# 96 instead of 80 row-gathered tokens, a ring of eight, and modulation products on four column groups

## Chip, cores and metric

One core of a Trainium2 chip runs the whole program. Times are device microseconds (us) of one execution; the kernel before takes 2507.22 us, the median of three runs (2506.68 to 2508.7). Engines are named as in the profile: PE (TensorE matmul), PEld (its weight loads), DVE (VectorE), ACT (ScalarE), POOL (GpSimd), SP (SyncE, which here only issues DMAs). A matmul of f32 operands stands in the trace as two records. All data is f32.

## What is computed

A first block (batch 1, 256 tokens, width 1024, with 256 context tokens), and then two layers of a second one. Cut to what matters here:

```python
# first block
s_lat, s_ctx = silu(c), silu(c_ctx)                    # two vectors of 1024
mod  = s_lat @ w_mod + b_mod                           # 1024 x 6144: shift, scale, gate, twice
cmod = s_ctx @ w_mod + b_mod
h = rms_norm(x) * (1 + sc1) + sh1                      # then projections, attention, Hyena, MLP
...
# each layer of the second block ends in peer_ffn
q = xn @ wq                                            # 8 heads x 2 x 128
scores = q . sub_keys;  top 16 of each half, top 16 of the 256 sums -> idx, gate (t, 8, 16)
act = einsum('td,thkd->thk', x, u_tab[idx])            # u_tab, v_tab: 16384 experts x 1024
y   = einsum('thk,thkd->td', gelu(act) * gate, v_tab[idx])
```

Each token uses 128 of the 16384 experts. Nothing else in the reference is touched by the change.

## The kernel before, in words

**The expert layer.** It is computed in two ways at once. The first TD = 176 tokens go the dense way on PE: all 16384 experts are multiplied with them, first `expert_scores` (u table, 128 expert blocks of 128, taken in 64 pairs, each pair 2 x 8 products of a 128x128 weight block with 176 columns), then `expert_values` (v table, 32 weight tiles of four blocks, 32 products of 176 columns each). The weights are streamed by SP in 2 MB tiles through three slots (`stream`, issued when the tile three places back was used up). A dense gate matrix comes from one-hot products: `gate_tiles(n)` makes the gates of BATCH = 4 tokens in four 128-column products, `onehots` (DVE) and `gate_onehots` (ACT) make their operands, `gates_out` (ACT), `gate_first` and `gate_second` (DVE) apply them. These run beside the pairs from pair FIRST_GATED = 20 on. A pair's PSUM bank is one of four and is freed by `gate_second`.

The last ROW_TOKENS = 80 tokens go the sparse way. POOL gathers rows with indirect DMAs (`gathers`): one gather brings 128 rows of 4 KB (16 tokens x 8 heads, one of the 16 choices), 80 of the u table and then 80 of the v table per layer, into a ring of RING = 6 buffers; gather m waits until the row work m - 6 is done. DVE makes a dot product of each u row set (`row_dots`, line 1892) and a scaled sum of each v row set (`row_sums`, line 1941). The dots stand in DVE's program between the gate work: DOTS_BEFORE = 12 before the first `onehots`, then DOTS_NUM / 2 = 1.5 for each pair, the rest at the end. The sums come after all gate work. `row_values(g)` lets PE add the sums of 16 tokens (eight products of 16 columns) between the tiles of the v stage. POOL's program is: the row tokens out and spread, the indices through DRAM (`move(0)`), the first RING + 2 gathers, the gates through DRAM (`move(1)`, it waits for DVE's `gate_ready`), all other gathers.

**The modulation.** w_mod is streamed in twelve 2 MB tiles. `modulation_rows(t)` makes eight products (one for each 128 rows of the contraction) of the two silu vectors (2 columns of weights) with 512 columns, all into partitions 0 and 1 of one PSUM bank. ACT copies them out (`modulation_row`), and `modulation_columns(t)` turns them with four transposes (line 481), which DVE takes (`modulation`). Tiles 0 to 3 stand at the start, 4 to 6 before the attention (behind `hy5`), 7 to 11 inside the attention loop at steps 0, 3, 6, 9 and 12. The order of work on each engine is written out by hand and does not depend on times.

The lines of the ring and the row dots:

```python
if m >= RING:
    pool.wait_ge(rows_used, m - RING + 1)
...
upto = min(ROWS, DOTS_BEFORE + (m + 1 - FIRST_GATED) * DOTS_NUM // 2)
row_dots(dots, upto - dots)
```

Of the kernel before, what the change touches and what calls it, by code (L numbers as in the profile page):

```python
# [19 lines left out]
ALU = mybir.AluOpType  # L20
# [5 lines left out]
P = 128  # L26
D = 1024
# [33 lines left out]
ROW_TOKENS = 80  # L61
# [4 lines left out]
RING = 6  # L66
# [5 lines left out]
ARENA = 46272  # L72
# [3 lines left out]
DOTS_BEFORE, DOTS_NUM = 12, 3  # L76
# [76 lines left out]
def build(nc, ins, out):  # L153
    ctx = ExitStack()
    with ctx:
# [21 lines left out]
        def const(n):  # L177
            c_at[0] += n
            return KON[:, c_at[0] - n:c_at[0]]
# [6 lines left out]
        SELG = const(GTOK)  # L186
        ZT = const(T)
        rstd = sb("rstd", [P, 2, T])
        small = sb("small", [P, 256])
# [18 lines left out]
        CE = take(KC, 2)  # L208
        MOD = take(48, 2)
# [62 lines left out]
        a_at[0] = wa_at + HALF * TD  # L272
# [7 lines left out]
        BA, BB, BP, BV, BI, BJ, GATE, EIDX = (take(TB * NSEL) for _ in range(8))  # L280
        assert a_at[0] <= wa_at + XTILES * TD
# [6 lines left out]
        XNS = view(wa_at + 48 * TD, D)  # L288
# [41 lines left out]
        def mod_rows(t):  # L330

            return SQF[0:2, 3072 + (t % 2) * 512:3584 + (t % 2) * 512] if t >= MODS_BEFORE_ATTENTION else \
                view(kt_at + A_COLS, 1024)[0:2, (t % 2) * 512:(t % 2 + 1) * 512]
# [23 lines left out]
        def _(pe):  # L357
# [110 lines left out]
            def modulation_rows(t):  # L468
                tile, w = weights(ins["w_mod"][t], KC * 512)
                w = w.rearrange("p (k n) -> p k n", k=KC)  # L470
                ps = begin(f"modr{t}")
                for k in range(KC):
                    last = mm(ps[0:2, :], CE[:, k, :], w[:, k, :], k == 0, k == KC - 1)
                used_up.append(tile)
                end(last, f"modr{t}")

            def modulation_columns(t):
                jobs.wait_read(pe, f"modr{t}")
                ps = begin(f"mod{t}")
                for j in range(4):  # L480
                    last = pe.transpose(ps[:, 2 * j:2 * j + 2], mod_rows(t)[:, j * P:(j + 1) * P],
                                        IDENT[0:2, 0:2])
# [456 lines left out]
        def _(act):  # L939
# [31 lines left out]
            def modulation_row(t):  # L971
# [3 lines left out]
                act.activation(mod_rows(t), bank(f"modr{t}")[0:2, :], ACT.Copy).then_inc(free(f"modr{t}"), 1)  # L975
# [292 lines left out]
        def _(dve):  # L1268
# [34 lines left out]
            dve.tensor_tensor(CE[:, :, :], CE[:, :, :], CS[:, :, :], ALU.mult).then_inc(s("silu_c_ready"), 1)  # L1303
# [823 lines left out]
def _constants():  # L2127
# [6 lines left out]
    for h in range(MLH):  # L2134
# [5 lines left out]
    rope = [x.reshape(TB, P, 32).transpose(1, 0, 2).reshape(P, TB * 32) for x in (np.cos(ang), np.sin(ang))]  # L2140
    iota = np.broadcast_to(np.arange(P, dtype=f), (P, P))
# [8 lines left out]
                             *rope, iota, selg, zt], axis=1).astype(f)  # L2150
# [72 lines left out]
```

## Time and profile before

| | |
|---|---|
| median of three runs | 2507.22 us |
| the profiled execution, own time | 2501.63 us |
| its span (first to last instruction) | 2499.8 us |
| PE busy | 2379.0 us (95%) |
| DVE, ACT, POOL busy | 1149.7, 454.4, 359.7 us |
| granted PE clock, mean | 0.962 of full |
| moved by DMA | 581.53 MB, mean 233 GB/s |

The span has these stretches: the first block up to 608 us (its modulation tiles in the first 330), then two layers of some 940 us. In the first of them the pairs of the u stage start at 883.6 us, the first gate product stands at 986.6, the v stage runs from 1232.8 to 1546.1; the second layer repeats this 942 us later. Busy shares are means over stages with different limits, so the stages are read one by one, and for each the question is which wait ends last there.

### The profile page before, as it was taken

Reading aid. Unit: us, or ns where it says so; the run is one execution under the profiler, and the core shown is the slowest. Engines: PE = TensorE matmul, PEld = TensorE weight load, DVE = VectorE, ACT = ScalarE, POOL = GpSimd, SP = SyncE. Lnnn points to the kernel's source line nnn. Section 1 sums busy time; section 2 is a strip of 40 time slices with the busy share of each in tenths; the row PEclk is TensorE's granted clock in tenths of the full one; section 3 lists DMA queues with packets and bytes.
Section 4 is the critical chain, followed back from the end, with each engine's and each line's share of the span. In section 5 each row is a group of like instructions: output and inputs, shape, how many; then the busy total and the mean of one; then the engine's idle time right before and its main releaser. Section 6 shows DMA issues by size and latency. Waiting matters only on the chain.

```text
span 2499.8 us, 32384 instructions
## 1 busy us (share of the span) xinstructions
PE 2379.0 (95%) x13376; PEld 2088.1 (84%) x13376; DVE 1149.7 (46%) x2391; ACT 454.4 (18%) x1076; POOL 359.7 (14%) x344
## 2 busy tenths in 40 slices
PE   6999879998989999999999998989999999999998
PEld 2464468887667899999999998667899999999998
DVE  2144422112532597667644410632597667644410
ACT  1112221000232112443200000232112443200000
POOL 0000000000000012333433300000012333433300
PEclk9999999999987999999999999987999999999999
DMA  8124222443421377989999973431368989899973
GB/s 314 66 88 183 101 85 101 152 152 128 157 101 51 135 270 297 340 316 346 332 410 409 409 264 119 165 126 51 127 229 325 336 315 345 331 407 409 409 283 118
DMA packets 103983, 581.53 MB, mean 233 GB/s; under 512 B 9145, under 2 KB 9529, under 8 KB 85786
## 3 DMA queue, kind: packets, MB, share of 16 engines
q1 hardware_dynamic: 55578, 403.31, 41.5%
q0 software_dynamic: 47968, 174.02, 19.1%
q8 instruction: 108, 1.77, 0.3%
q10 hardware_dynamic: 288, 2.10, 0.2%
q14 instruction: 41, 0.34, 0.0%
HBM read 577.52 MB, written 1.87 MB: 232 GB/s over the span
## 4 chain that ended last, share of the span: by engine, by line
PE 92%; DVE 2%; ACT 2%; DMA 2%; issue 1%; POOL 0%; POOLq 0%; SPq 0%; DVEq 0%; ACTq 0%
PE psum L387 90%; PE psum L422 1%; DMA arena<-in_w_mod 1%; DMA bounce<-arena 1%; DMA arena<-in_peer_u,small 1%; ACT HT L1074 0%; DVE rstd L1621 0%; DVE arena L1474 0%; POOL arena L2036 0%; POOLq L2009 0%; DVE XT L1993 0%; SPq L2062 0%; ACT arena L1156 0%; ACT arena L1159 0%; ACT arena L1150 0%
## 5 line engine op out<-in xcount | busy, mean ns | idle before, releaser
L387 PE MATMUL psum<-arena 128*128 128x176 f32 (+6 forms) x6154 | 1053.2, 334 | 22.1 <-DVE arena L1744 9.6
L387 PE MATMUL psum<-HT,arena 128*128 128x176 f32 (+1 forms) x5984 | 1043.2, 335 | 14.8 <-DVE HT L1623 7.1
L387 PEld LDWEIGHTS psum<-HT,arena 128*128 128x128 f32 x5984 | 972.4, 191 | 66.7 <-issue 16.7
L387 PEld LDWEIGHTS psum<-arena 128*128 128x128 f32 (+1 forms) x6154 | 913.7, 192 | 132.2 <-issue 108.3
L1941 DVE SCALAR_TENSOR_TENSOR arena<-arena,small 128x1024 f32<-128x1024 f32 x150 | 192.8, 1285 | 214.2 <-DMA arena<-in_peer_v,small 214.0
L2036 POOL DMA_INDIRECT arena<-in_peer_u,small x160 | 188.1, 1175 | 407.1 <-DVE small L1892 374.7
L387 PE MATMUL psum<-arena,HT 128*128 128x384 f32 (+3 forms) x544 | 199.2, 527 | 18.1 <-ACT HT L1003 11.1
L1892 DVE CUSTOM_DVE_ANT_0 arena<-arena 128x1024 f32<-128x1024 f32 x160 | 191.0, 1220 | 18.9 <-DMA arena<-in_peer_u,small 17.3
L2036 POOL DMA_INDIRECT arena<-in_peer_v,small x160 | 158.7, 992 | 257.0 <-DVE arena L1941 230.6
L387 PEld LDWEIGHTS psum<-arena,HT 128*128 128x128 f32 x544 | 106.8, 198 | 104.1 <-issue 42.4
L951 ACT ACTIVATE arena<-psum 128x512 f32<-128x512 f32 (+6 forms) x130 | 64.9, 513 | 693.5 <-PE psum L422 355.9
L2042 POOL DMA_DIRECT2D row_tokens<-arena x2 | 1.3, 640 | 1275.6 <-ACT arena L951 1275.6
L1228 ACT ACTIVATE arena<-arena 128x128 f32<-128x128 f32 x352 | 112.3, 390 | 170.9 <-DVE arena L1901 170.9
L1901 DVE TENSOR_TENSOR arena<-arena,KON 128x1024 f32<-128x1024 f32 x88 | 107.0, 1217 | 0.0
L387 PE MATMUL psum<-arena,KON 128*128 128x256 f32 (+5 forms) x252 | 73.3, 441 | 26.9 <-ACT arena L1099 16.8
L387 PEld LDWEIGHTS psum<-arena,KON 128*128 128x128 f32 (+1 forms) x252 | 55.0, 241 | 48.1 <-ACT arena L1099 17.3
L1993 DVE TENSOR_TENSOR XT<-psum,XT 128x512 f32<-128x512 f32 x8 | 5.0, 683 | 189.4 <-PE psum L387 189.4
L1916 DVE TENSOR_TENSOR arena<-psum,arena 128x168 f32<-128x168 f32 (+21 forms) x88 | 65.4, 743 | 51.6 <-ACT arena L1235 50.7
L1575 DVE TENSOR_SCALAR arena<-psum,arena 128x256 f32<-128x256 f32 x22 | 12.0, 544 | 167.4 <-PE psum L387 167.0
L1099 ACT ACTIVATE arena<-XT 128x512 f32<-128x512 f32 x16 | 9.4, 623 | 394.7 <-POOLq L2009 340.7
L1927 DVE TENSOR_TENSOR arena<-psum,arena 128x352 f32<-128x352 f32 (+41 forms) x86 | 30.4, 354 | 106.4 <-ACT arena L1218 97.7
L1218 ACT ACTIVATE arena<-psum 128x352 f32<-128x352 f32 (+20 forms) x124 | 44.7, 361 | 164.6 <-PE psum L387 164.6
(225 smaller groups left out, 986.5 us busy)
## 6 DMA issues: line engine op xcount, KB each, us to landing
arena<-in_peer_ut SPq DMA_DIRECT2D x64, 2048.0 KB, 8.4
arena<-in_peer_v SPq DMA_DIRECT2D x64, 2048.0 KB, 16.4
arena<-in_w_mod SPq DMA_DIRECT2D x12, 2048.0 KB, 8.1
arena<-in_w_in SPq DMA_DIRECT2D x16, 1536.0 KB, 6.2
arena<-in_w_up SPq DMA_DIRECT2D x11, 2048.0 KB, 8.0
arena<-in_peer_wq SPq DMA_DIRECT2D x8, 2048.0 KB, 7.2
arena<-in_w_out SPq DMA_DIRECT2D x6, 2048.0 KB, 7.3
arena<-in_w_down SPq DMA_DIRECT2D x11, 1024.0 KB, 4.8
```

Of the source, the lines that this page charges most:

```text
L387: return pe.matmul(o, a, b, start=start, stop=stop, skip_group_check=True)
L422: last = pe.transpose(ps[0:rows, j * P:(j + 1) * P], part, IDENT)
L951: act.activation(dst, src, ACT.Copy).then_inc(psum_free[jobs.where[name][0]], 1)
L1218: last = act.activation(WA[:, 2 * m:2 * m + 2, done:TD], ps[:, :, done:TD], ACT.Gelu_apprx_tanh)
L1228: last = act.activation(rows, rows, ACT.Copy, scale=SELT[:, 2, at:at + 1])
L1575: steps(dve.tensor_scalar(a, src, col("fcw", FC + c), col("fcb", c), ALU.mult, ALU.add))
L1892: dve.tensor_tensor_reduce(out=GR[j], in0=GR[j], in1=XNG[:, g % 2, :], scale=1.0, scalar=0.0, op0=ALU.mult, op1=ALU.add, accum_out=ACTV[:, ...
L1901: dve.tensor_tensor(OH[:, 2 * (n % 2):2 * (n % 2) + 2, :, :], bc(SELT[:, 0:2, at:at + BATCH].unsqueeze(3), P, 2, BATCH, P), bc(IOTA.unsque ...
L1916: dve.tensor_tensor(w, ps[:, :].rearrange("p (x i) -> p x i", x=BATCH)[:, :, 0:2 * m], w, ALU.mult).then_inc(free(f"g{n}"), 1)
L1927: dve.tensor_tensor(w, ps[:, :, 0:done], w, ALU.mult).then_inc(free(f"u{m}"), 1)
L1941: dve.scalar_tensor_tensor(y, GR[j], w, y, ALU.mult, ALU.add).then_inc(rows_used, 1)
L2036: pool.indirect_dma_start(out=GR[j], out_offset=None, in_=rows, in_offset=bass.IndirectOffsetOnAxis(ap=EG[:, n:n + 1].bitcast(U32), axis=0 ...
```

## The change

Three constants of the row work move: ROW_TOKENS 80 to 96 (so TD 176 to 160, six row groups instead of five, 96 gathers of each table and layer, and 40 gate groups instead of 44), RING 6 to 8, DOTS_NUM 3 to 4 (two dots a pair). Buffers move to make room. The modulation products use four column groups of PE: the silu vectors are padded to 32 columns (`CE4`), product k goes to columns and PSUM partitions 32 (k mod 4) on, so that two products add up in each group, and the four partial sums are added when the rows are turned: `modulation_columns` multiplies all 128 partitions with a 0/1 matrix `PAIR` of two columns.

```diff
-ROW_TOKENS = 80
+ROW_TOKENS = 96
-RING = 6
+RING = 8
-DOTS_BEFORE, DOTS_NUM = 12, 3
+DOTS_BEFORE, DOTS_NUM = 12, 4
...
+        PAIR = const(2)
...
-        small = sb("small", [P, 256])
+        small = sb("small", [P, 3 * ROWS])
...
+        CE4 = take(KC, 32)
...
-            return SQF[0:2, 3072 + (t % 2) * 512:3584 + (t % 2) * 512] if t >= MODS_BEFORE_ATTENTION else \
-                view(kt_at + A_COLS, 1024)[0:2, (t % 2) * 512:(t % 2 + 1) * 512]
+            return SQF[:, 3072 + (t % 2) * 512:3584 + (t % 2) * 512] if t >= MODS_BEFORE_ATTENTION else \
+                view(kt_at + A_COLS, 1024)[:, (t % 2) * 512:(t % 2 + 1) * 512]
...
                 for k in range(KC):
-                    last = mm(ps[0:2, :], CE[:, k, :], w[:, k, :], k == 0, k == KC - 1)
+                    q = 32 * (k % 4)
+                    last = pe.matmul(ps[q:q + 32, :], CE4[:, k, :], w[:, k, :], start=k < 4, stop=k >= KC - 4,
+                                     tile_position=(0, q))
...
                 for j in range(4):
-                    last = pe.transpose(ps[:, 2 * j:2 * j + 2], mod_rows(t)[:, j * P:(j + 1) * P],
-                                        IDENT[0:2, 0:2])
+                    last = mm(ps[:, 2 * j:2 * j + 2], mod_rows(t)[:, j * P:(j + 1) * P], PAIR, j == 0, True)
...
-                act.activation(mod_rows(t), bank(f"modr{t}")[0:2, :], ACT.Copy).then_inc(free(f"modr{t}"), 1)
+                act.activation(mod_rows(t), bank(f"modr{t}")[:, :], ACT.Copy).then_inc(free(f"modr{t}"), 1)
...
-            dve.tensor_tensor(CE[:, :, :], CE[:, :, :], CS[:, :, :], ALU.mult).then_inc(s("silu_c_ready"), 1)
+            steps(dve.memset(CE4[:, :, :], 0.0))
+            dve.tensor_tensor(CE4[:, :, 0:2], CE[:, :, :], CS[:, :, :], ALU.mult).then_inc(s("silu_c_ready"), 1)
```

PE at the start of the program, the four modulation tiles before the attention's projections, before the change:

```order
L387 MATMUL psum<-arena 2x512 x8
L387 MATMUL psum<-KON,arena 64x256
L387 MATMUL psum<-arena 2x512 x8
L481 MATMUL psum<-KON,arena 128x2 x4
L387 MATMUL psum<-arena 2x512 x8
L481 MATMUL psum<-KON,arena 128x2 x4
L387 MATMUL psum<-arena 2x512 x8
L481 MATMUL psum<-KON,arena 128x2 x8
```

The same place after the change:

```order
L476 MATMUL psum<-arena 32x512 x8
L389 MATMUL psum<-KON,arena 64x256
L476 MATMUL psum<-arena 32x512 x8
L389 MATMUL psum<-KON,arena 128x2 x4
L476 MATMUL psum<-arena 32x512 x8
L389 MATMUL psum<-KON,arena 128x2 x4
L476 MATMUL psum<-arena 32x512 x8
L389 MATMUL psum<-KON,arena 128x2 x8
```

Nothing moved: each product of 2 rows became one of 32 rows in its own column group, and the transposes became plain products.

POOL in one layer, from the index move to the first v gathers, before (L2036 is a gather, L2014 and L2017 the two halves of a move through DRAM, L2023 the spread of a group's tokens):

```order
L2036 DMA arena<-in_peer_u,small 128x1024 x8
L2014 DMA bounce<-arena 80x128
L2017 DMA small<-bounce 128x5x16
L2036 DMA arena<-in_peer_u,small 128x1024 x13
L2023 DMA arena<-row_tokens 128x1x1024
L2036 DMA arena<-in_peer_u,small 128x1024 x16
```

After (L2040, L2018, L2021 and L2027 are the same four):

```order
L2040 DMA arena<-in_peer_u,small 128x1024 x10
L2018 DMA bounce<-arena 96x128
L2021 DMA small<-bounce 128x6x16
L2040 DMA arena<-in_peer_u,small 128x1024 x13
L2027 DMA arena<-row_tokens 128x1x1024
L2040 DMA arena<-in_peer_u,small 128x1024 x16
```

Ten gathers instead of eight now stand ahead of the gate move.

DVE at the first gate groups of a layer, before (L1892 a row dot in two instructions, L1901 `onehots`, L1916 `gate_first`, L1927 `gate_second`):

```order
L1901 TENSOR_TENSOR arena<-arena,KON 128x1024 x2
L1916 TENSOR_TENSOR arena<-psum4,arena 128x4x42
L1901 TENSOR_TENSOR arena<-arena,KON 128x1024
L1916 TENSOR_TENSOR arena<-psum5,arena 128x4x42
L1901 TENSOR_TENSOR arena<-arena,KON 128x1024
L1891 REGISTER_ALU
L1892 ISA arena,small<-arena 128x1024
L1892 ISA small 128x1
L1927 TENSOR_TENSOR arena<-psum1,arena 128x2x8
L1916 TENSOR_TENSOR arena<-psum6,arena 128x4x44
```

After (L1896, L1905, L1920 and L1931 are the same four):

```order
L1905 TENSOR_TENSOR arena<-arena,KON 128x1024 x2
L1920 TENSOR_TENSOR arena<-psum4,arena 128x4x42
L1905 TENSOR_TENSOR arena<-arena,KON 128x1024
L1896 ISA arena,small<-arena 128x1024
L1896 ISA small 128x1
L1896 ISA arena,small<-arena 128x1024
L1896 ISA small 128x1
L1931 TENSOR_TENSOR arena<-psum1,arena 128x2x4
L1920 TENSOR_TENSOR arena<-psum5,arena 128x4x44
L1905 TENSOR_TENSOR arena<-arena,KON 128x1024
```

One gate group instead of two stands behind pair 20, and every pair carries two dots where it carried one or two in turn.

## Rows read from the trace of the kernel before

**Rows 1.** The page, part 4: the chain that ended last, share of the span by engine.

```profile
PE 92%; DVE 2%; ACT 2%; DMA 2%; issue 1%; POOL 0%; POOLq 0%; SPq 0%; DVEq 0%; ACTq 0%
```

**Rows 2.** Windows: PE, PEld, DVE, ACT, POOL busy (count), PEclk, DMA share, GB/s.

```profile
221.40:329.00 107.60, 93.94 (x404) 47.76 (x404) 49.16 (x136) 29.86 (x70) 0.00 (x0) 0.97 0.26 98
986.60:1232.80 246.20, 246.19 (x1728) 246.19 (x1729) 167.81 (x256) 97.85 (x300) 78.11 (x68) 0.99 0.89 331
1232.80:1448.00 215.20, 215.20 (x1457) 215.20 (x1455) 103.81 (x93) 1.09 (x6) 77.13 (x78) 1.00 1.02 406
```

**Rows 3.** Groups by form, PE, first 620 us: records | busy us, mean ns.

```profile
L387 PE MATMUL psum<-arena 128*2 128x512 f32 x192 | 85.9, 602 | 3.7 <-DMA arena<-in_w_mod 3.7
```

**Rows 4.** Timeline of PE, start of program: start us, length, records [idle before].

```profile
23.12 8.72 PE L387 MATMUL psum<-arena 128*2 128x512 f32 x16 [3.68 <-DMA arena<-in_w_mod]
...
46.94 7.03 PE L387 MATMUL psum<-arena 128*2 128x512 f32 x16
...
66.75 13.13 PE L387 MATMUL psum<-arena,HT 128*128 128x384 f32 x32 [11.12 <-ACT HT L1003]
```

**Rows 5.** Line 2071, landing of the third w_mod tile (issued 7.2) and fourth (31.9).

```profile
DMA to landing us min/median/max: 25.6/25.6/25.6
...
DMA to landing us min/median/max: 8.1/8.1/8.1
```

**Rows 6.** Timeline of PE and DVE, end of the projections and start of attention.

```profile
193.35 13.89 PE L387 MATMUL psum<-arena 128*2 128x512 f32 x32
...
202.93 1.49 DVE L1452 TENSOR_TENSOR arena<-arena 128x1280 f32<-128x1280 f32 x1
...
221.44 1.95 PE L387 MATMUL psum<-arena 64*128 64x512 f32 x6 [1.10 <-issue]
```

**Rows 7.** Timeline of PE, attention steps 3 (with a modulation tile) and 4 (without).

```profile
241.72 0.66 PE L422 MATMUL psum<-KON,arena 128*128 128x128 f32 x4
...
251.36 0.66 PE L422 MATMUL psum<-KON,arena 128*128 128x128 f32 x4
...
254.17 0.66 PE L422 MATMUL psum<-KON,arena 128*128 128x128 f32 x4
```

**Rows 8.** PE: one score product (timeline), two in different row groups (by form, 302.5:303.8).

```profile
234.68 1.12 PE L387 MATMUL psum<-arena 64*128 64x512 f32 x2
...
L387 PE MATMUL psum<-arena 64*128 64x512 f32 x4 | 1.1, 642 | 0.0
```

**Rows 9.** Timeline of PE: a pair, a gate group, a row group's eight products.

```profile
1115.69 4.94 PE L387 MATMUL psum<-HT,arena 128*128 128x176 f32 x32
1120.46 1.05 PE L387 MATMUL psum<-arena 128*128 128x128 f32 x8
...
1446.50 1.85 PE L387 MATMUL psum<-KON,arena 128*128 128x16 f32 x16
```

**Rows 10.** DMA queues from 1260 to 1420 us: weights q1, gathers q0; packets, MB, share.

```profile
q1 hardware_dynamic: 8569, 34.05, 53.3%
q0 software_dynamic: 8572, 31.21, 49.0%
```

**Rows 11.** Line 2071: landing of v tiles issued at 1261.9 and, 17 later, 1427.8.

```profile
DMA to landing us min/median/max: 15.8/15.8/15.8
...
DMA to landing us min/median/max: 18.1/18.1/18.1
```

**Rows 12.** Timeline: dot 8, first onehots, first gate products.

```profile
979.05 1.23 DVE L1892 CUSTOM_DVE_ANT_0 arena<-arena 128x1024 f32<-128x1024 f32 x1 [7.50 <-DMA arena<-in_peer_u,small]
...
984.02 2.36 DVE L1901 TENSOR_TENSOR arena<-arena,KON 128x1024 f32<-128x1024 f32 x2
...
986.61 3.68 PE L387 MATMUL psum<-arena 128*128 128x128 f32 x16 [2.12 <-ACT arena L1228]
```

**Rows 13.** Timeline of DVE, late in the u stage, the turn after a pair with two dots.

```profile
1206.22 0.49 DVE L1927 TENSOR_TENSOR arena<-psum,arena 128x320 f32<-128x320 f32 x1 [0.62 <-ACT arena L1218]
```

**Rows 14.** Timeline of POOL: the first v gather of layer one.

```profile
1228.66 0.93 POOL L2036 DMA_INDIRECT arena<-in_peer_v,small  x1 [0.30 <-issue]
```

More of the change, by code:

```diff
@@ L71 @@
 GBATCHES = TD // BATCH
-ARENA = 46272
+ARENA = 46204
 MAIN = WSLOTS * WSIZE + 4096
@@ L271, in build @@
         QP = view(wa_at, 16, T)
-        a_at[0] = wa_at + HALF * TD
+        a_at[0] = wa_at + 48 * TD
         SC = take(TB, 16 * NK)
@@ L280, in build @@
         BA, BB, BP, BV, BI, BJ, GATE, EIDX = (take(TB * NSEL) for _ in range(8))
+        XNS = take(D)
         assert a_at[0] <= wa_at + XTILES * TD
@@ L287, in build @@
         SELT = take(3, T)
-        XNS = view(wa_at + 48 * TD, D)
         YP = [view(oh_at, D), view(oh_at + D, D), XNG[:, 0, :], XNG[:, 1, :]]
@@ L2140, in _constants @@
     rope = [x.reshape(TB, P, 32).transpose(1, 0, 2).reshape(P, TB * 32) for x in (np.cos(ang), np.sin(ang))]
+    pair = (i[:, None] % 32 == np.arange(2)[None, :]).astype(f)
     iota = np.broadcast_to(np.arange(P, dtype=f), (P, P))
@@ L2149, in _constants @@
     consts = np.concatenate([np.eye(P), np.ones((P, P)), -np.ones((P, P)), le, lt, nge, erow.reshape(P, -1),
-                             *rope, iota, selg, zt], axis=1).astype(f)
+                             *rope, iota, selg, pair, zt], axis=1).astype(f)
     deltas = np.linspace(math.log(1e-2) / 1.5, math.log(1e-2) / 0.3, HY)
```

## The prediction

> **What bounds it now.** I read the chain of the page first: PE holds 92% of it [rows 1], so PE's own work is the time, and what takes columns off PE gains unless something else is late right behind. Then the windows of the two long stages. In the u stage PE is busy all 246 us, with DMA at 0.89 and 331 GB/s; in the first 215 us of the v stage PE is busy throughout as well, but DMA stands at 1.02 and 406 GB/s [rows 2]: a second engine is full there. That is the point on which the larger half of the change hangs. In the first block the modulation costs 85.9 us of PE for 96 products, 0.87 us each before they overlap anything [rows 3].
>
> **Fewer dense columns: the price.** A pair is 16 products of 176 columns and takes 1120.46 - 1115.69 = 4.77 us, 298 ns each (its row says 4.94, since the last product runs 0.17 us into the next row); a gate group, four products of 128 columns, takes 1.05 - 0.17 = 0.89 us, 222 ns each [rows 9]. So 1.58 ns a column, 25.3 ns for 16 columns, and a product of 160 takes 273 ns. A pair becomes 4.37 us, a v tile 8.74. Each stage has 1024 such products a layer: 25.9 us on paper, four times in all. I now take the stages apart.
>
> *Up to pair 20.* 21 pairs would give 8.5 us, but the first gate products wait for ACT and behind it DVE's first `onehots` at 984.02, which stands after dot 11; dots 8 to 11 ran from 979.05, after 7.5 us of waiting for a gather that was queued behind the gate move [rows 12]. PE would only wait longer. But now ten gathers stand ahead of the move, and only dots 10 and 11 are left for after it: two dots of 1.2 us come off, **2.5 us**. The two gathers wait for dots 0 and 1, which are done before the gates are ready, so the move behind them is not held up.
>
> *Pairs 21 to 63.* 43 x 16 x 25.3 ns = 17.4 us, and four gate groups fewer, 3.6 us: 21.0. Against it: a pair with its gate group takes 5.26 us instead of 5.66, and DVE's turn late in the stage with two dots fills all but 0.62 us of 5.66 [rows 13]; it needs about 5.05, so it fits by 0.2 us. And the gathers: two for 5.26 us (512 KB each, 199 GB/s) and a 2 MB tile for 10.5 us (199 GB/s) are 398 GB/s, under the 406 seen in the v stage [rows 2] by 2%. Two close fits let some waits through; the ring of eight covers single late landings, not a rate. From nothing to 8.6 us (if a gather takes the 2.74 us of the v stage, a pair takes 5.48: 43 x 0.2); I take 3.5. **17.5 us**.
>
> *v stage.* While the v gathers run, the weights queue and the gather queue moved 8569 and 8572 packets in the same 160 us [rows 10]: as good as one each in turn. The tiles were issued every (1427.8 - 1261.9) / 17 = 9.76 us, and yet their landing grew from 15.8 to 18.1 us [rows 11], 0.14 us a tile: the weights queue was always behind and gave a tile in 9.9 us. With three slots PE meets it when landing reaches two tiles' time, which is 19.1 us now and 17.5 with 160 columns. So there PE is paced by DMA at 9.9 us a tile, whatever its columns, for as long as gathers run. That is 80 gathers from 1228.7 [rows 14] to about 1448, 2.74 us each; 96 take 263 us, to 258 us into the stage. In these pass 258 / 9.9 = 26 tiles, and one more from the lead at the start; the other five run free at 8.74, 44 us, with two row groups of 1.7 us [rows 9]: 305 us against 313.3 now. I take **7 us** (the other 19 go into waiting for weights). The ends: 0 (26 tiles at 10.2) and 24 (no waiting, one more row group).
>
> Of rules on this: the Trainium skill, DMA: Bandwidth & Descriptors, section Queues, rings and completion order, says that an engine goes round between the queues that have work, a packet at a time. By that rule the weights cannot get more than half the packets while gathers are queued, and a deeper ring takes nothing more; the packet counts above agree. Without it the stage would give 24 us, the fourth case below.
>
> Per layer 2.5 + 17.5 + 7 = 27 us, **54 us** for two. Costs nothing: the larger token and index moves (POOL waits for dots anyway), 16 more dots and sums (DVE idle 78 of 246 and 111 of 215 us [rows 2]).
>
> **The modulation.** Eight products take 7.03 us [rows 4]. Whether four column groups work at once no row shows. The nearest are the two scores of a head, which lie in two row groups: both took 1.1 us where one takes 1.12 [rows 8], so two f32 products of 512 columns run in the time of one. If four column groups do the same, eight products are two rounds: 0.87 x 2 and a little, 1.9 us, 5.1 less. The ends are 7.0 (one after another) and 1.9; 3.6 would be two at a time. I take 1.9, from the row that is nearest. The turning becomes four products with full weights, near the 0.21 us of a 16-column one [rows 9]: 0.85 instead of 0.34 us, 0.5 more a tile.
>
> The Trainium skill, TensorE: Matmul & The Clock Gate, section Part 3, gives 3.07 times for four row groups and 2.38 for three column groups. An estimate by it is 7.03 / 3.07 = 2.3 us a tile, 3 us less gain over the program; no run here shows it.
>
> *Tiles 0 to 3.* The first still starts when it lands, 23.1. The third lands at 7.2 + 25.6 = 32.8, the fourth was issued at 31.9, when the first was used up, and landed at 40.0 [rows 5]; issued five us earlier it stands behind the others and lands near 39.5. So the fourth product set starts at 39.5 instead of 46.94 [rows 4] and is 5.1 shorter: 12.5, less 1.5 for a PE that has idled and may be at its lower clock. The chain from there to the projections at 66.75 keeps its length. **11 us**, and 10 if the groups work two at a time, since the landing sets it.
>
> *Tiles 4 to 6.* 15 us on paper, from 221.44. But the transposes of the context keys wait for DVE, whose last step ends at 204.4 [rows 6], and the slot of the last of these three tiles is freed by the last projection product at 193.4 [rows 6], so it lands 8 us later, at 201.4; its products, then the transposes and ACT's copies (some 8 us) come after. Scores start near 211. **10 us**.
>
> *Tiles 7 to 11.* A step with a tile takes 251.36 - 241.72 = 9.64 us, one without 2.81 [rows 7]; so a step less 5.1 is still above what ACT and DVE need for a step. Five times 4.6 less 2 for a lower clock in an emptier loop: **21 us**. The zeroing of CE4 (under 0.3 us) ends before 23 us, ACT's copies take the same time for 128 partitions.
>
> **Sum.** 54 + 42 = 96 us off 2501.6 of the profiled execution: 2405.6. That one lay 5.6 under the median, so 2411 us.
>
> **Rivals.**
> 1. *The column groups don't overlap* (the change doesn't do what it says). Then 42 us go and 12 x 0.5 are added: 2459 us. For it: groups share all 128 rows, the scores do not. Against: rows 8. 15%.
> 2. *The weights get less than half.* At 45 of 100 packets a tile takes 11.3 us and a gather 2.42: 96 end after 227 us of the stage, 20 tiles, the other 11 take 96, the stage 323, worse than now. 34 us more in two layers: 2445. The equal counts speak against. 10%.
> 3. *Slower than before.* PE now waits some 1.1 us in each of 27 tiles; if the chip took the clock down for it, products would take what they took at the lower of two levels after the wait before 986.6: eight of 128 columns in 3.68 us, 460 ns instead of 222 [rows 12]. A tile is 17.5 us then, 7.6 more than its 9.9; 54 tiles, 410 us if all. It eats the 96 us once 23% of the stretch is at the low level; at a third of it the time is 2548. Against: in the attention PE idles 13.7 of 107.6 us, an eighth, in short pieces, and the granted clock there was 0.97 [rows 2]; here it would be a tenth. 5%.
> 4. *DMA yields.* Weights land in time: the v stage gives 24 instead of 7: 2377 us. 7%.
>
> **Numbers.** Forecast 63%: 2411, in itself 2390 to 2432 from the ends of u and v stage and of the modulation. Case 1 lies within the range to 2462, so does case 2; outside are case 4, case 3 and tails of the forecast: 2386 to 2462. A difference under 0.2% (5 us) cannot be told from none; faster 94%, same 1%, slower 5%.
>
> **What would show it.** In the changed profile: products of 160 columns near 273 ns in the u stage; PE waits in front of v tiles by the weights' DMA, some 20 us a layer, all before the gathers end, and tile issues 9.9 us apart; the first gate product 2 to 3 us sooner after the indices; modulation sets of 1.9 us at line 476; attention from 221 to 329 shrunk by 21. It is wrong if the sets take 7 us, if PE waits for one-hots in the u stage by more than 8 us a layer, or if the granted clock drops in the v stage.

## The result

The changed kernel takes **2418.94 us** (median of 4 runs, 2413.75 to 2422.23) against 2507.44 us before (4 runs, 2506.68 to 2508.7): a ratio of 0.9645, interval 0.9627 to 0.9663. The forecast was 2411 us, with a range of 2386 to 2462. The profiled execution is the fastest of the four, with its own time at 2413.75 us and a span of 2411.9; the profile of before had 2501.63 and 2499.8. So 87.9 us of span are to be explained, where the sum gave 96.

The chain of the page after, which answers to [rows 1], says what changed. PE had 92% of it; now it has 65%, DMA holds a fifth and DVE a tenth:

```profile
PE 65%; DMA 20%; DVE 10%; ACT 2%; issue 2%; POOL 1%; SPq 0%; POOLq 0%; DVEq 0%; ACTq 0%
PE psum L389 63%; DMA arena<-in_peer_v 13%; DMA arena<-in_peer_u,small 5%; DVE arena L1836 2%; DMA arena<-in_w_mod 2%; DVE arena L1834 1%; PE psum L424 1%; DVE arena L1839 1%; PE psum L476 1%; POOL arena L2040 1%; DVE arena L1869 1%; DMA bounce<-arena 1%; DVE arena L1875 1%; DVE arena L1879 0%; DVE arena L1896 0%
```

The windows of the attention, of layer one's u stage, of its v stage while v gathers run, and of layer two's u stage, after (columns as in [rows 2]; the second window runs 3.3 us into the v stage):

```profile
202.80:296.50 93.70, 71.49 (x425) 46.29 (x425) 55.44 (x146) 33.66 (x74) 0.00 (x0) 0.91 0.32 122
945.18:1175.10 229.92, 228.12 (x1721) 227.88 (x1722) 185.09 (x292) 88.85 (x286) 113.28 (x90) 0.99 1.00 395
1175.10:1425.00 249.90, 235.15 (x1706) 230.31 (x1704) 117.84 (x99) 0.00 (x0) 82.67 (x88) 1.00 1.02 408
1862.93:2093.20 230.27, 226.68 (x1696) 226.20 (x1697) 182.31 (x288) 87.01 (x279) 111.71 (x89) 0.98 1.00 392
```

The u stage went from a DMA share of 0.89 and 331 GB/s to 1.00 and 395, the v stage stayed at 1.02, and there PE is now busy 235 of 250 us instead of throughout.

**The modulation.** The timeline of PE, which answers to [rows 4 and 6]; line 476 is a tile's eight products, in 16 records:

```profile
22.98 2.69 PE L476 MATMUL psum<-arena 128*32 128x512 f32 x16 [3.76 <-DMA arena<-in_w_mod]
...
32.69 1.92 PE L476 MATMUL psum<-arena 128*32 128x512 f32 x16 [0.52 <-DMA arena<-in_w_mod]
...
40.25 3.64 PE L476 MATMUL psum<-arena 128*32 128x512 f32 x16 [4.66 <-DMA arena<-in_w_mod]
43.83 2.25 PE L389 MATMUL psum<-KON,arena 128*128 128x2 f32 x16
...
57.77 12.44 PE L389 MATMUL psum<-arena,HT 128*128 128x384 f32 x32 [11.12 <-ACT HT L1006]
...
202.81 1.95 PE L389 MATMUL psum<-arena 64*128 64x512 f32 x6 [1.10 <-issue]
```

A set takes 1.92 us where it took 7.03. The projections start at 57.77 instead of 66.75 (9.0 gained), the scores at 202.81 instead of 221.44 (18.6 in all), and the first product behind the attention at 296.50 instead of 337.65 (41.2 in all).

**The u stage.** A pair and a gate group after, which answer to [rows 9]:

```profile
1031.86 4.51 PE L389 MATMUL psum<-HT,arena 128*128 128x160 f32 x32
1036.20 1.05 PE L389 MATMUL psum<-arena 128*128 128x128 f32 x8
```

The pair is 1036.20 - 1031.86 = 4.34 us. From the first gate product to the first v product 226.6 us pass in layer one (945.18 to 1171.8) and 230.3 in layer two, against 246.3 and 246.1.

**The v stage.** The timeline of PE, early in the stage and where the v gathers end:

```profile
1198.49 8.96 PE L389 MATMUL psum<-arena 128*128 128x160 f32 x64 [0.41 <-DMA arena<-in_peer_v]
1208.42 8.96 PE L389 MATMUL psum<-arena 128*128 128x160 f32 x64 [0.97 <-DMA arena<-in_peer_v]
1218.17 8.96 PE L389 MATMUL psum<-arena 128*128 128x160 f32 x64 [0.79 <-DMA arena<-in_peer_v]
...
1425.68 26.35 PE L389 MATMUL psum<-arena 128*128 128x160 f32 x192 [0.86 <-DMA arena<-in_peer_v]
1451.86 1.85 PE L389 MATMUL psum<-KON,arena 128*128 128x16 f32 x16
```

Each tile is 8.8 us of work and starts 9.75 to 9.93 us behind the one before it, waiting for its weights; from 1425.68 on, when the gathers have ended (the last is issued at 1404.78 and they take some 20 us), three tiles run in one piece, and after a row group the last three. PE's waits in the stage, layer one:

```profile
PE psum L389 <- DMA arena<-in_peer_v: 15.4, 19, 1.6
```

The queues in 1180 to 1420 us, which answer to [rows 10]:

```profile
q1 hardware_dynamic: 12953, 51.46, 53.7%
q0 software_dynamic: 12759, 46.45, 48.6%
```

Still one packet each, 12953 and 12759, though the bytes differ by a tenth. From the first v product to the end of the last the stage takes 308.1 us in layer one and 306.8 in layer two, against 312.8 and 312.9 before (the 313.3 that the prediction started from is 0.5 too long).

### The profile page after: what moved, and what is told of

It is laid out like the page before. It is cut to its first block, busy times and chain, and to the rows that moved or that the text cites. A ratio compares the mean times of both kernels' runs of the same rounds, so it can differ in the third digit from the quotient of the medians.

```text
span 2411.9 us, 32515 instructions
## 1 busy us (share of the span) xinstructions
PE 2229.7 (92%) x13392; PEld 1977.1 (82%) x13392; DVE 1210.2 (50%) x2474; ACT 432.7 (18%) x1036; POOL 444.7 (18%) x410
## 4 chain that ended last, share of the span: by engine, by line
PE 65%; DMA 20%; DVE 10%; ACT 2%; issue 2%; POOL 1%; SPq 0%; POOLq 0%; DVEq 0%; ACTq 0%
PE psum L389 63%; DMA arena<-in_peer_v 13%; DMA arena<-in_peer_u,small 5%; DVE arena L1836 2%; DMA arena<-in_w_mod 2%; DVE arena L1834 1%; PE psum L424 1%; DVE arena L1839 1%; PE psum L476 1%; POOL arena L2040 1%; DVE arena L1869 1%; DMA bounce<-arena 1%; DVE arena L1875 1%; DVE arena L1879 0%; DVE arena L1896 0%
## 5 line engine op out<-in xcount | busy, mean ns | idle before, releaser
L389 PE MATMUL psum<-HT,arena 128*128 128x160 f32 (+1 forms) x5984 | 990.5, 326 | 14.6 <-DVE HT L1627 7.1
L389 PE MATMUL psum<-arena 128*128 128x160 f32 (+6 forms) x5898 | 915.8, 317 | 70.6 <-DMA arena<-in_peer_v 29.8
L389 PEld LDWEIGHTS psum<-HT,arena 128*128 128x128 f32 x5984 | 922.8, 191 | 66.7 <-issue 16.6
L389 PEld LDWEIGHTS psum<-arena 128*128 128x128 f32 (+2 forms) x5898 | 835.4, 195 | 128.2 <-issue 42.4
L1945 DVE SCALAR_TENSOR_TENSOR arena<-arena,small 128x1024 f32<-128x1024 f32 x180 | 231.2, 1285 | 248.6 <-DMA arena<-in_peer_v,small 248.3
L2040 POOL DMA_INDIRECT arena<-in_peer_u,small x192 | 242.9, 1265 | 303.4 <-DVE small L1896 257.5
L1896 DVE CUSTOM_DVE_ANT_0 arena<-arena 128x1024 f32<-128x1024 f32 x192 | 228.1, 1220 | 54.0 <-DMA arena<-in_peer_u,small 52.6
L2040 POOL DMA_INDIRECT arena<-in_peer_v,small x192 | 187.8, 978 | 313.8 <-DVE arena L1945 269.4
L1905 DVE TENSOR_TENSOR arena<-arena,KON 128x1024 f32<-128x1024 f32 x80 | 97.3, 1218 | 0.0
L1920 DVE TENSOR_TENSOR arena<-psum,arena 128x168 f32<-128x168 f32 (+19 forms) x80 | 63.7, 796 | 37.2 <-ACT arena L1238 37.1
L1834 DVE MAX8 arena<-arena 128x8 f32<-128x128 f32 (+1 forms) x192 | 51.7, 324 | 48.5 <-ACT arena L954 47.8
L1221 ACT ACTIVATE arena<-psum 128x320 f32<-128x320 f32 (+39 forms) x122 | 41.7, 342 | 142.1 <-PE psum L389 142.1
L424 PEld LDWEIGHTS psum<-KON,arena 128*128 128x128 f32 x192 | 26.2, 166 | 45.0 <-DVE arena L1478 18.6
```

The source lines that it names most:

```text
L389: return pe.matmul(o, a, b, start=start, stop=stop, skip_group_check=True)
L424: last = pe.transpose(ps[0:rows, j * P:(j + 1) * P], part, IDENT)
L1221: last = act.activation(WA[:, 2 * m:2 * m + 2, done:TD], ps[:, :, done:TD], ACT.Gelu_apprx_tanh)
L1834: done[n] = steps.later(dve.max(out=v, in_=values))
L1896: dve.tensor_tensor_reduce(out=GR[j], in0=GR[j], in1=XNG[:, g % 2, :], scale=1.0, scalar=0.0, op0=ALU.mult, op1=ALU.add, accum_out=ACTV[:, ...
L1905: dve.tensor_tensor(OH[:, 2 * (n % 2):2 * (n % 2) + 2, :, :], bc(SELT[:, 0:2, at:at + BATCH].unsqueeze(3), P, 2, BATCH, P), bc(IOTA.unsque ...
```

## The experiments

**Each part alone.** First the modulation with 80 tokens, ring of six and three dots for two pairs as before:

```diff
-ROW_TOKENS, RING, DOTS_NUM = 96, 8, 4
+ROW_TOKENS, RING, DOTS_NUM = 80, 6, 3
```

> The changed kernel with the row work put back: 80 tokens, ring of six, three dots in two pairs. My theory (the two halves of the change don't touch each other; the modulation gave 41.2 us in the changed trace, since first-block rows stand 8.98 us earlier at the projections, 18.6 at the first scores and 41.2 at the end of the attention): 2507 - 41 = 2466 us. Rival (part of the 41 us is a gift of something else in the first block, or the gain is given back in the second block): over 2475 us.

Measured 2470.65 us (2463.76 to 2476.68), ratio 0.9862 (0.9838 to 0.9886): 4.7 above the theory and below the rival. Its u stages last 246.1 and 247.4 us, its v stages 313.0 and 312.8: what is not touched is as before, and the gain lies ahead of the first retrieval product, which comes 42 us sooner.

Then the rows with the modulation of before:

```diff
-q = 32 * (k % 4)
-last = pe.matmul(ps[q:q + 32, :], CE4[:, k, :], w[:, k, :], ..., tile_position=(0, q))
+last = mm(ps[0:2, :], CE[:, k, :], w[:, k, :], k == 0, k == KC - 1)
```

> The changed kernel with the modulation put back to two-column products and transposes. Theory: only the second block's gain is left, 24.6 and 22.3 us in the two layers of the changed trace: 2507 - 47 = 2460 us, first-block rows as before. The two parts alone should add up to the whole, 88 us, within 4 us. Rival (the parts help each other): together over 8 us less than the whole.

Measured 2465.78 us (2455.64 to 2468.91), ratio 0.9828 (0.9797 to 0.9858), 5.8 above the theory. The waits of PE in its first v stage:

```profile
PE psum L389 <- DMA arena<-in_peer_v: 14.2, 16, 2.2
```

The waits for v weights come with the rows, not with the modulation. The parts give 37 and 42 us by the medians, 79 together, the whole 88. That is 9 apart where I had expected at most 4, and more than the 8 that I had set for the rival, parts that help each other. The profiles show by stretches where the 9 are. Up to the first retrieval product the modulation alone is 42.1 us ahead of before and the whole kernel 41.1; from there to the end of layer two's v stage the rows alone take 1561.5 us and the whole 1557.7, against 1604.7 before. That makes 42.1 + 43.2 = 85 of 88. What the medians lack beyond that lies in stretches that the single edits don't touch: the first block of the rows-only run is 5.5 us longer than the same code before, and from the first retrieval product to the end of layer two's v stage the modulation-only run is 5.3 us longer. Why these are longer no run shows; an interaction of the parts is not needed for the 9, and one of up to 3 us is not excluded.

**Is it the size of the packets that paces the v weights?** The same table of v weights, its rows laid out beforehand such that a tile is 16 KB in a row for each partition, not four pieces of 4 KB:

```diff
-ins["peer_v_2"].rearrange("l e d -> (l e) d")[...].rearrange("(a j) d -> j a d", a=4)
+ins["peer_vt_2"][bass.ds(layer * (XQ * P) + q * P, P), :]
```

> The changed kernel, but the v weights come from a copy of the table in which the 16 KB of a partition stand together, so that a tile is 128 pieces of 16 KB instead of 512 of 4 KB; bytes, products and gathers stay. Theory (in the v stage the two queues are served a packet in turn, and the weights lose because their packets are no larger than the gathers'): the waits for weights, 15 us in layer one, go, the v stage falls from 308 to about 288 us, gathers end later, tile landing falls under 15 us: 2419 - 40 = 2379 us (2370 to 2390). Rival (it is the DMA engines' total rate of 409 GB/s that is missing, whoever gets it): the same 9.9 us a tile and the same time, 2415 to 2423 us.

Measured 2392.09 us (2379.34 to 2397.16), ratio 0.9548 (0.9522 to 0.9573), 2 above the range of the theory; a second time 2384.06 (below), inside it. The first 250 us of the v stage in the windows, and the queues from 1180 to 1420 us:

```profile
1174.50:1425.00 250.50, 250.50 (x1858) 250.50 (x1857) 110.18 (x94) 1.06 (x7) 105.28 (x87) 1.00 1.02 419
```

```profile
q1 hardware_dynamic: 3847, 55.95, 55.1%
q0 software_dynamic: 12133, 44.16, 45.9%
```

PE is busy in all 250.50 us. The weights moved 56 instead of 51.5 MB in the same time with 3847 instead of 12953 packets, the gathers 44.2 instead of 46.5. Both v stages last 287.3 us, 20 less. So of the 4.5 MB that the weights gained about half came from the gathers and about half from a total that rose from 409 to 418 GB/s. The rival, a fixed total of 409 GB/s whoever gets it, would have left the waits; but the rise alone would not have removed them: a tile each 8.73 us and the gathers of before want 240 and 194 GB/s, 434 together. What is shown is that the size of the pieces changes who gets the bytes. Turns of one packet rest on the equal counts of the two kernels with 4 KB pieces; this run does not test them, since its tiles are issued every 8.7 us, at PE's pace, and the weights queue is no longer always behind.

**The same edit in the kernel before**, where PE never waited for a v tile:

```diff
-ins["peer_v_2"].rearrange("l e d -> (l e) d")[...].rearrange("(a j) d -> j a d", a=4)
+ins["peer_vt_2"][bass.ds(layer * (XQ * P) + q * P, P), :]
```

> The kernel before, with one edit: the v weights are read from a copy of the table in which a tile is 16 KB in a row for each partition (128 pieces) instead of 4 KB (512 pieces). Theory (a queue gets one packet in turn, so bigger pieces give the weights a larger share; in the kernel before PE never waited for a v tile, so the share has nothing to give): v stage 313 us unchanged, gathers end later, total 2507 within 5, against the 27 us that the same edit gave the changed kernel. Rival (bigger pieces make DMA cheaper in general, and PE or DVE gain everywhere from it): some us faster, 2485 to 2500.

Measured 2508.83 us against 2507.59, ratio 1.0004 (0.9993 to 1.0015). A v tile lands after 10.8 us instead of 17.0 (medians of 1260 to 1420 us), DMA moves 419 GB/s instead of 409, and nothing comes of it: both v stages last 312.8 us.

```profile
q1 hardware_dynamic: 2368, 34.60, 51.1%
q0 software_dynamic: 8853, 32.23, 50.2%
...
arena<-in_peer_vt SPq DMA_DIRECT2D x16, 2048.0 KB, 10.8
```

**Is the u stage bound by DMA?** Ten dots instead of twelve ahead of the first one-hots, so that the gates can start sooner. ACT's first gate batch of a layer also waits for the first leg of the gate move: of twelve dots the last two need gathers that POOL issues behind the move, of ten none does:

```diff
-DOTS_BEFORE, DOTS_NUM = 12, 4
+DOTS_BEFORE, DOTS_NUM = 10, 4
...
+if n == 0:
+    act.wait_ge(s("gate_moved"), layer * 32 + 16)
```

> The changed kernel with 10 instead of 12 dots before the first one-hots, so that these no longer wait for the first gather behind the gate move. Theory A (DMA binds the u stage: share 1.00 and 395 GB/s there, so dots come when their rows come): the first gate products stand 10 us earlier, but the gain is lost to later waits for gathers in the u stage, at most 4 us of a layer are left: 2411 to 2419 us. Theory B (the wait of 10.8 us before the first gate product is PE's own loss): 20 us less, 2399 us.

Measured 2414.13 us (2408.26 to 2423.26), ratio 0.9641 (0.9612 to 0.967), 4.8 us below the changed kernel, within the spread of either. PE's first gate product, and DVE's waits for peer rows in the u stage of this run and then of the changed kernel:

```profile
936.30 1.05 PE L389 MATMUL psum<-arena 128*128 128x128 f32 x8
```

```profile
DVE arena L1898 <- DMA arena<-in_peer_u,small: 47.7, 24, 5.0
```

```profile
DVE arena L1896 <- DMA arena<-in_peer_u,small: 15.0, 9, 6.4
```

The gates start 8.9 us sooner with no idle time before them, the stage lasts 235.5 us instead of 226.6, and the v stage begins at the same 1171.83 in both. The waiting only moved from one place ahead of the gates to DVE's dots, which now wait 47.7 us for their rows. In layer two the gates start 8.9 us sooner and the stage is 3.4 longer (233.7 against 230.3), so there 5.5 are kept. Of 17.8 us in two layers 12.3 are given back, and the medians differ by 4.8: theory A, though 5.5 is more than the 4 us that it left to a layer.

**Fewer dots instead**, three for two pairs:

```diff
-DOTS_BEFORE, DOTS_NUM = 12, 4
+DOTS_BEFORE, DOTS_NUM = 12, 3
```

> The changed kernel with 3 dots for every two pairs instead of 4 (as in the kernel before): the u stage's one-hots then consume gathers more slowly, so its DMA engines are less loaded and more of the v gathers go into the v stage. Theory (u stage paced by DMA's bytes): the u stages lose their 5 to 8 us of waits and last 219 to 222 us instead of 226.6 and 230.3; the v gathers begin later by about 20 us and last until after the last tile, so the v stage's free tail shrinks and the row sums wait at its end: 2419 or up to 10 us more. Rival (waits of the u stage are DVE's or ACT's own): the u stages do not change, the end loses 10 us a layer, 2440.

Measured 2436.07 us (2432.9 to 2441.3), ratio 0.9709 (0.9693 to 0.9725). The u stage, and PE's waits in the v stage of layer one:

```profile
954.60:1179.80 225.20, 225.19 (x1701) 225.20 (x1702) 161.99 (x248) 90.85 (x281) 78.33 (x69) 0.99 0.96 359
```

```profile
PE psum L389 <- DVEq L1948: 12.9, 1, 12.9
PE psum L389 <- DMA arena<-in_peer_v: 11.8, 14, 1.7
```

The window runs 0.6 us into the v stage. PE never waits inside the u stages now, DMA is at 0.96, and 224.6 and 224.8 us are what their products alone take. So the changed kernel loses 2.0 us there in layer one and 5.5 in layer two, and my 219 to 222 was too low. The price is at the other end: the v gathers end late, the row sums hold PE for 12.9 us, and the v stages last 320.3 and 320.0 us. The theory was right that the waits go and missed the total (2419 to 2429) by 7 us; the rival had them stay and came nearer with the total and with what the end costs. The sum is 17 us worse than the changed kernel.

**How deep must the ring be?**

```diff
-RING = 8
+RING = 6
```

> The changed kernel with a gather ring of six instead of eight. Theory (the gathers of the u stage are paced by the bytes that the DMA engines move, and in the v stage by one packet in turn, so depth only moves where they wait): u stage within 2 us of 226.6 and 230.3, v stage within 2 us of 308.3 and 307, total 2419 within 6. Rival (the depth is what lets DVE run without waits; single late landings reach PE): DVE's waits for peer rows grow, one-hots late, 5 to 15 us more in the two u stages, 2424 to 2434. The gates move two gathers earlier in POOL's order as well, which could give back up to 2 us of the first gate product.

Measured 2433.97 us (2431.12 to 2439.25), ratio 0.9702 (0.9685 to 0.9719): 15 us slower than the changed kernel. My theory falls, and the rival's 2424 to 2434 holds. The u stages last 233.2 and 233.1 us, and the first gate product comes 105.1 us behind the first retrieval product instead of 102.9; the v stages are as they were. DVE's waits for peer rows in layer one's u stage, to be set against the 15.0 us above:

```profile
DVE arena L1896 <- DMA arena<-in_peer_u,small: 36.4, 20, 4.2
```

Six buffers also mean two gathers fewer ahead of the gates' move. The next experiment keeps the eight and takes back only these two.

**The two gathers ahead of the move.**

```diff
-gathers("peer_u_2", 0, RING + 2)
+gathers("peer_u_2", 0, RING)
 pool.wait_ge(s("gate_ready"), 1)
 move(1, GATE, GG, "gate_moved")
-gathers("peer_u_2", RING + 2, ROWS - RING - 2)
+gathers("peer_u_2", RING, ROWS - RING)
```

> The changed kernel with eight gathers instead of ten ahead of the move of the gates on POOL. In the changed kernel gathers 8 and 9 are issued at 918.8 and 920.8, the gates are ready in the same moment, so the move starts 1.9 us late (922.73), takes 8.2 us, and dot 10 waits until 940.17. Theory (what the two gathers give, two dots done early, they take again by holding up the move): with the move first it starts 1.9 us sooner, gathers 8 and 9 are issued behind it and their dots come behind as well, and the first gate product starts within 1 us of where it does now after the indices; total 2419 within 5. Rival (the two early gathers are worth their two dots of 1.2 us, as predicted): the first gate product comes 2 to 3 us later, 4 to 6 us in the program, about 2424.

Measured 2430.44 us (2429.35 to 2432.14), ratio 0.9693 (0.9677 to 0.9709): 11.5 us slower than the changed kernel. My theory falls here too; the rival had the mechanism and half the size. POOL in the changed kernel and then in this run; line 2040 is a gather, 2018 and 2021 are the two legs of the move:

```profile
918.83 1.67 POOL L2040 DMA_INDIRECT arena<-in_peer_u,small  x1 [32.02 <-DVE small L1896]
920.80 1.92 POOL L2040 DMA_INDIRECT arena<-in_peer_u,small  x1 [0.30 <-issue]
922.73 0.59 POOL L2018 DMA_DIRECT2D bounce<-arena  x1
930.92 0.87 POOL L2021 DMA_DIRECT2D small<-bounce  x1 [7.60 <-DMA bounce<-arena]
932.10 0.99 POOL L2040 DMA_INDIRECT arena<-in_peer_u,small  x1 [0.30 <-issue]
```

```profile
923.63 0.58 POOL L2018 DMA_DIRECT2D bounce<-arena  x1 [33.06 <-DVE arena L1963]
930.35 0.87 POOL L2021 DMA_DIRECT2D small<-bounce  x1 [6.14 <-DMA bounce<-arena]
931.53 0.99 POOL L2040 DMA_INDIRECT arena<-in_peer_u,small  x1 [0.30 <-issue]
```

The first gate product comes 105.1 and 105.5 us behind the first retrieval product, 2.2 and 2.8 later than in the changed kernel: that is the two dots that the prediction priced at 2.5. The u stages are longer as well, 232.1 and 234.1 us, by 5.5 and 3.8. In a stage whose dots wait for transfers, two gathers that move while POOL would wait for the gates anyway are two gathers less later. The ring of six has the same loss: its u stages take 233.2 and 233.1 us and this run's 232.1 and 234.1, though DVE's waits for rows are 36.4 us there and 21.5 here. The 3.5 us by which it is slower still are all that depth as such is worth here, and no more than the spread of the runs.

**Does the order of the column groups matter?** Neighbouring products in the same group:

```diff
-q = 32 * (k % 4)    # start=k < 4, stop=k >= KC - 4
+q = 32 * (k // 2)   # start=k % 2 == 0, stop=k % 2 == 1
```

> The changed kernel, but the eight modulation products of a tile go to the four column groups in another order: two neighbours in the same group (0,0,1,1,2,2,3,3) instead of 0,1,2,3,0,1,2,3. The work is the same and the result too. Theory A (TensorE takes products in order, and one overlaps only a neighbour in another column group): with 0.87 us for a product alone, the set is five steps, 0 | 0,1 | 1,2 | 2,3 | 3, so 4.3 us instead of 1.9; 2.4 us for each of 12 tiles, 29 us, of which some 5 are hidden by waits for the landing of tiles: about 2443 us (2435 to 2450). Theory B (the groups hold their own queues, order does not matter): sets of 1.9 us and the time of the changed kernel, 2419 within 5.

Measured 2422.39 us (2415.32 to 2425.73), ratio 0.9664 (0.9645 to 0.9683). A set at low clock and one at full clock, in the timeline of PE:

```profile
33.34 3.66 PE L476 MATMUL psum<-arena 128*32 128x512 f32 x16
...
207.97 1.94 PE L476 MATMUL psum<-arena 128*32 128x512 f32 x16
```

1.94 us in this order, 1.92 in the other. Theory A, 4.3 us, falls: with two products in each group it does not matter which of these two orders they come in. Other splits over the groups no run tried.

**The best of both.** Wide pieces and ten dots, in a first comparison and then again beside wide pieces alone on one chip:

```diff
+ins["peer_vt_2"][bass.ds(layer * (XQ * P) + q * P, P), :]
+DOTS_BEFORE, DOTS_NUM = 10, 4
+act.wait_ge(s("gate_moved"), layer * 32 + 16)    # first gate batch, as above
```

> The changed kernel with both earlier edits: v weights in pieces of 16 KB, and ten dots instead of twelve ahead of the first one-hots. In the v stage PE no longer waits, so the DMA engines have slack there; the u stage is still bound by bytes. Theory (u stage bound by DMA: what the gates gain by starting 9 us sooner, the stage gives back by half or more): within 5 us of the run with wide pieces alone, 2387 to 2394. Rival (the gain of the early start holds since the late gathers now find room in the v stage): 2375 to 2382.

> The run with v weights in pieces of 16 KB once more, beside the next one on the same chip, to compare the two. Theory: 2385 to 2395, the next one 5 to 9 us below it (its second layer was 5.2 us shorter in the profiles, 898.4 against 903.6 us from the end of one v stage to the end of the next). Rival (the 20 us between their medians of two calls are real): 15 us or more between them.

> Wide pieces and ten dots once more on the same chip as the run with wide pieces alone. Theory: 5 to 9 us below that one. Rival: 15 us or more below it.

The first comparison gave 2371.52 us (2367.72 to 2379.33; ratio 0.9452, 0.9435 to 0.9468), below what both theories said. Side by side, wide pieces alone take 2384.06 (2378.57 to 2386.97; 0.9499, 0.9482 to 0.9516) and with ten dots 2380.25 (2378.93 to 2383.27; 0.9489, 0.9473 to 0.9505). The difference of 3.8 us, a little under the 5 to 9 of the theory, is within the spread of the times, and the rival of 15 us is out. The stretches of the two profiles say the same as the medians: the gates start 10.7 us sooner in each layer, the u stages are 6.6 and 10.9 us longer, and 3.9 are kept. The same kernel with ten dots took 2371.52 us the first time and 2380.25 the second, so a difference of some 9 us between two of these medians is not by itself an effect. PE's waits from the first gate product to the end of the v stage in these two runs, wide alone first, in which 10.5 us are the wait ahead of the gates:

```profile
PE psum L389 <- ACT arena L1230: 15.4, 4, 10.5
```

```profile
PE psum L389 <- ACT arena L1230: 10.4, 6, 4.9
```

No wait for v weights is left in either. Both beat the changed kernel by 35 to 39 us.

## Why the prediction held, and where it did not

The forecast of 2411 us was 8 us too low, 0.3%, and the case it named came in: the mechanisms were right, with the terms ahead of pair 20 and of the v stage too large.

*Modulation, 42 us: measured 41.2.* The sets run in 1.92 us at full clock; the choice of the low end by [rows 8] was right, and rival 1 is dead. By the Trainium skill, TensorE: Matmul & The Clock Gate, section Part 3, the estimate had been 2.3 us a set; the measured 1.92, 3.7 times less than 7.03, is better than either of its ratios. By parts: tiles 0 to 3 gave 9.0 instead of 11, since the fourth set started at 40.25 and not at 39.5, took 3.64 us, and the turning behind it 2.25. These are the lengths of the low clock (the same set is 1.92 at 32.69), after 4.66 us without work. The allowance of 1.5 us was about enough for the set and left out the turning. Tiles 4 to 6 gave 9.6 of 10. Tiles 7 to 11 gave 22.5 instead of 21: 116.2 us from the first scores to the first product behind the attention became 93.7. The granted clock there fell from 0.97 [rows 2] to 0.91, with PE busy 71 of 94 us. That the three parts miss in both directions (-2.0, -0.4, +1.5) and their sum by 1 us only is luck.

*Up to pair 20, 2.5 us: measured 0.3 in layer one (first gate product 41.4 us sooner, of which 41.1 came from ahead) and 0.8 in layer two.* The row that the term stood on was right, two dots off, and the run without the two early gathers shows their 2.2 and 2.8 us. The failing step is the sentence "so the move behind them is not held up": in the changed kernel the move follows the issue of gather 9 without a pause, 80.4 us behind the first retrieval product, and without the two gathers it starts at 78.8, when the gates are ready. That is 1.6 us. Then the first leg of the move lasted 8.2 us from issue to the next leg against 7.5 before, and dot 10 ran 8.1 us behind the issue of its gather where dot 8 had run 6.7 behind [rows 12]:

```profile
940.17 1.22 DVE L1896 CUSTOM_DVE_ANT_0 arena<-arena 128x1024 f32<-128x1024 f32 x1 [8.74 <-DMA arena<-in_peer_u,small]
```

```profile
945.18 2.08 PE L389 MATMUL psum<-arena 128*128 128x128 f32 x8 [10.76 <-ACT arena L1231]
```

How much of that is chance is open: the first leg took 4.8 us in the rows-only run, where the first gate product came 97.7 us behind the first retrieval product instead of 102.9, and 8.6 in the modulation-only run, whose gather order is that of before.

*Pairs 21 to 63, 17.5 us: measured 19.6 and 15.8.* The 21.0 us of products were nearly exact: with three dots PE runs the stages in 224.6 and 224.8 us without a wait, 21.7 and 21.3 less than before. The waits, taken at 3.5, were 2.0 and 5.5. Of the two close fits the queues were the tight one (DMA share 1.00, 395 GB/s): with two fewer dots ahead of the gates DVE waits 47.7 us for rows and the stage is longer, with fewer dots a pair and DMA at 0.96 PE waits no more.

*v stage, 7 us: measured 4.7 and 6.1.* The pace was foreseen, 9.9 us a tile: the 23 tiles from 1198.49 to 1425.68 took 9.88 each, then six ran free. The failing step is "one more from the lead at the start". The three tiles before 1198.49 ran at 8.9 us, a lead of a third of a tile and not of one: the queue was full in the u stage already, so the tile that is issued as the stage begins, at 1172.2, lands after 16.5 us, where the one issued at 1233.2 took 9.7 before:

```profile
DMA to landing us min/median/max: 16.5/16.5/16.5
```

```profile
DMA to landing us min/median/max: 9.7/9.7/9.7
```

In the free end there were six tiles instead of five, and the gathers ended 4 us sooner in the stage than forecast, which gave most of it back. PE loses 15.4 us in its 19 marked waits; by the starts of the tiles it is about 20, near the 19 that the sum took. The rule of the Trainium skill that the prediction weighed (DMA: Bandwidth & Descriptors, Queues, rings and completion order: a packet at a time, in turn) agrees with 12953 against 12759 packets.

*"Costs nothing: the larger token and index moves".* They cost no time of the program, but the index move is slower. The second leg of the index move took 2.5 us for 80 tokens and 7.1 for 96, so POOL's first gather is issued 4.4 us later:

```profile
876.63 1.01 POOL L2040 DMA_INDIRECT arena<-in_peer_u,small  x1 [7.06 <-DMA small<-bounce]
```

It is 7.1 in the ring of six as well, 6.6 in the rows-only run and 2.5 in the modulation-only run, so it goes with the tokens. Nothing comes of it, since DVE reaches its first dot some 40 us later.

*The sum.* Up to the first retrieval product 41.1, from there to the end of layer one's v stage 24.7, from there to the end of layer two's 22.3: 88.1, where the span shows 87.9 and the forecast was 96. The 8 missing are 7 in the layers (47 instead of 54) and 1 in the modulation.

*The rivals.* Column groups that don't overlap: dead, 1.92 us. Weights with less than half of the packets: dead, 12953 of 25726. (Its tile of 11.3 us should have been 9.9 x 50 / 45 = 11.0 and its gather 2.74 x 50 / 55 = 2.49; the case would have come to some 2438 us, also within the range.) A clock that falls in the v stage: dead, 1.00 there, with PE idle 15.4 us in 19 waits. DMA that yields by itself: no; but laid out in wide pieces the stage lasts 287.3 us, 25.5 less than before where that rival had said 24, and the kernel 2384 to 2392 us where it had said 2377.

## What to carry to other kernels

When PE's share of the chain is above 90%, price each stage also against the engine that is second: of 25.5 us that PE could save in a v stage (312.8 to 287.3, with wide pieces), 20.8 were lost to waits for weights in layer one, where DMA stood at 1.02. Where two queues share full DMA engines, look at packets as well as bytes, and try larger pieces on the queue that is waited for; this gave 27 to 35 us here and nothing where nobody waited. And in a stage bound by transfers, a transfer that can be issued during an earlier wait can be worth its own time again later: two gathers gave 11.5 us, of which only 5 by the work that they unlock.

## What the runs showed that I had not expected

- Products in four column groups overlap in both orders that were run: eight f32 products of 512 columns in 1.94 us with neighbours in the same group, 1.92 with neighbours in different ones, where products over all 128 rows in one group took 7.03.
- The time of one and the same kernel goes with the mean granted clock of the run. The changed kernel took 2413.75 us at 0.954, 2418.25 and 2419.64 at 0.950, 2422.23 at 0.947. In the profiles it is the first block that differs: its first retrieval product starts at 842.3 us in the changed kernel and at 852.5 with the ring of six, which is not in use by then, and the windows of the attention show it. The changed kernel and then the ring of six:

```profile
200.00:330.00 130.00, 105.57 (x589) 76.37 (x588) 58.86 (x154) 41.69 (x91) 0.00 (x0) 0.92 0.30 114
```

```profile
200.00:330.00 130.00, 105.72 (x587) 77.98 (x586) 58.26 (x153) 43.98 (x95) 0.00 (x0) 0.89 0.30 115
```

  So 10 us between two profiles can come with the clock, in a stretch that the edit does not touch, and stages were compared here by their lengths and not by when they start. What decides the clock from run to run is open.
- The small move of 96 tokens' indices through DRAM took 6.6 to 7.6 us on its second leg and that of 80 tokens 2.5. Why is open; no run separates the number of tokens from the layout that goes with it.
